# Splitting the weight stream three units ahead, with low parts written over the raw weights

## The chip, the cores and the metric

The kernel runs on one core of a Trainium2 chip. The metric is device time in microseconds (us) of one execution. TensorE (PE) multiplies, PEld is its weight load, VectorE (DVE) and ScalarE (ACT) do elementwise work, GpSimd (POOL) and SyncE (SP) here mostly issue DMA transfers.

## The reference

One token sequence (256 tokens, width 2048) passes through two transformer-like blocks. Nearly all arithmetic is in matrix products with float32 weights:

```python
def first_block(x, ...):
    h = rmsnorm(x, ln1_w)
    z, xbc, dt_raw, q, k, v, f_raw = jnp.split(h @ w_in, split_at, axis=-1)
    x = x + jnp.concatenate([ssd_group(...), fox_group(...)], axis=-1) @ w_out
    x = x + peer(rmsnorm(x, ln2_w), peer_wq, peer_k1, peer_k2, peer_u, peer_v)
    return rmsnorm(x, lnf_w)

def peer(h, wq, k1, k2, u, v):      # 16384 experts, 8 heads, 16 picks each
    s1, s2 = ...                    # scores of h @ wq against two sets of keys
    v1, i1 = lax.top_k(s1, 16); v2, i2 = lax.top_k(s2, 16)
    sc, pos = lax.top_k(all sums v1 + v2, 16)
    act = gelu(u[idx] . h)          # idx: the picked experts
    return sum(softmax(sc) * act * v[idx])

def second_block(x, mem, ...):      # attention + convolution, cross attention, MLP
    h = h + jnp.square(jax.nn.relu(nm @ w1[l])) @ w2[l]
```

The kernel computes the experts' part densely for 208 of the 256 tokens (all 16384 experts, gated by a sparse table) and by gathered rows for the other 48.

## The kernel before, in words

All weight matrices are laid out as one stream of 532 units of 128 x 2048 float32 (1 MB each). A unit gives PE 16 tiles of 128 x 128 to multiply with. To keep float32 accuracy, every unit is split: ACT copies it to a rounded high part (`w_hi`, helper `hi`, line 672; its caller in the units with two matmuls per tile cuts it in 1536 and 512 columns, lines 685 and 691), DVE subtracts to get the low part (`w_lo`, helper `lo`, line 1117), and PE multiplies with both.

Buffers before: `raw` has four slots of 1 MB, `w_hi` and `w_lo` two each. SP loads unit u+4 into the slot of unit u as soon as `split_done` shows unit u split (line 521). ACT and DVE split unit u+2 in the helper `ahead(u)`, which waits for `mm_done` of unit u, since unit u+2 takes the buffers that PE has just finished with. PE waits at the start of each unit for `split_done` and `bank_free`.

Every engine runs its instructions in the order in which the program is written. Stages in the order of the stream, with the stage names of the table `STREAM`: `xbc`, `v1`, `z`, `qk1`, `out1` (first mixing block), `wq` (queries; DVE does the top-k in between), `u0` (first 2048 experts, DVE goes on with the top-k), `u1` (DVE builds the one-hot tiles `pick_a`, `pick_b` for the gate table, PE multiplies them in `gate_group`, ACT evicts them), `e0`, `e1`, then six rounds `u2`, `e2` ... `u7`, `e7`. In those rounds POOL gathers expert rows (1 MB each) for the 48 tokens, two buffers, and DVE handles one gathered block in a `job` at fixed units. `job(0)` stands after unit 3 of `u2` and waits for `set_rows`, two broadcast loads issued at the start of `u2`. In a round's `u` stage ACT copies a bank (L950), applies Gelu (L954) and writes the high part of the gated activation (`cast`, L942), DVE adds (L1601), gates (L1555) and writes the low part (`act_lo`, L1616). In unit 0 of the following `e` stage PE waits tile by tile for them: its tile 15 needs `act_lo` of unit 15 (`gated_tile`). In `e` stages DVE accumulates (L1594, L1595). Then come the stages of the second block, the last eight of which (`up`, `down`) are the MLP.

The order of ACT's work in unit k of a `u` stage is, in full:

```python
ahead_first(u)
eng.wait_ge(mm_done, u + 1)
eng.wait_ge(tmp_split, n - 3)
eng.activation(tmp[:, j, 0:TD], bank[j][:, TD:2 * TD], ACT.Copy).then_inc(pair_copied, 1)
if k < 15:
    ahead_rest(u)
eng.wait_ge(pair_sum, 16 * (r - 2) + k + 1)
eng.activation(tmp[:, j, 0:TD], tmp[:, j, 0:TD], ACT.Gelu).then_inc(tmp_full, 1)
if k >= 1:
    cast(r, k - 1)
if k == 15:
    ahead_rest(u)
    cast(r, 15)
```

Of the kernel before, what the change touches and what calls it, by code (L numbers as in the profile page):

```python
# [21 lines left out]
P = 128  # L22
D = 2048
T = 256
# [5 lines left out]
SPLIT = 2  # L30
# [97 lines left out]
def build(nc, x_in, mem_in, stream, cols_in, consts_in, rows_in, wide_in, wdtf_in, keys_in,  # L128
          rel_in, onehot_in, u_rows, v_rows, out):
    ctx = ExitStack()  # L130
    with ctx:
# [19 lines left out]
        w_hi = [sb(f"w_hi{i}", [P, UNIT], F32R) for i in range(SPLIT)]  # L151
        w_lo = [sb(f"w_lo{i}", [P, UNIT], F32R) for i in range(SPLIT)]
# [131 lines left out]
        mm_part = sem("mm_part")  # L284
# [160 lines left out]
        PART = 3 * UNIT // 4  # L445

# [64 lines left out]
        def _(sp_eng):  # L511
# [154 lines left out]
        def _(act):  # L666
            eng = nc.scalar

            def hi(landed, k):

                eng.wait_ge(raw_full[k % RAW], landed)
                eng.activation(w_hi[k % SPLIT][:, :], raw[:, k % RAW, :], ACT.Copy).then_inc(hi_done, 1)  # L672
# [7 lines left out]
            def ahead_first(u):  # L680

                k = u + 2
                eng.wait_ge(mm_part, u - UNIT0["e0"] + 1)
                eng.wait_ge(raw_full[k % RAW], 16 * (k // RAW + 1))
                eng.activation(w_hi[k % SPLIT][:, 0:PART], raw[:, k % RAW, 0:PART], ACT.Copy)  # L685

            def ahead_rest(u):

                k = u + 2
                eng.wait_ge(mm_done, u + 1)  # L690
                eng.activation(w_hi[k % SPLIT][:, PART:UNIT], raw[:, k % RAW, PART:UNIT], ACT.Copy).then_inc(hi_done, 1)  # L691
# [89 lines left out]
            for j in range(SPLIT):  # L781
                hi(16, j)
# [146 lines left out]
            for name in ("e0", "e1"):  # L929
                for k in range(16):  # L930
                    ahead_first(UNIT0[name] + k)
                    ahead_rest(UNIT0[name] + k)
# [11 lines left out]
            for r in range(2, PEER_ROUNDS):  # L944
                for k in range(16):
                    u, n, j = UNIT0[f"u{r}"] + k, BQ[f"u{r}"] + k, k % 4
                    ahead_first(u)
# [3 lines left out]
                    if k < 15:  # L951
                        ahead_rest(u)
# [4 lines left out]
                    if k == 15:  # L957
                        ahead_rest(u)
# [20 lines left out]
            for j in range(16):  # L979
# [6 lines left out]
                ahead_first(UNIT0["e7"] + j)  # L986
                ahead_rest(UNIT0["e7"] + j)
# [109 lines left out]
            for j in range(14):  # L1097
                ahead(u0 + j)
# [11 lines left out]
        def _(dve):  # L1110
# [135 lines left out]
            for j in range(SPLIT):  # L1246
# [606 lines left out]
            for j in range(16):  # L1853
                if j % 4 == 3:
                    add_chunk((j // 4) * 512, (j // 4) % 2, u0 + j + 1, stat[:, 14:16])
                if j < 14:
# [13 lines left out]
        def _(pe):  # L1870
# [3 lines left out]
            def feature_unit(j, act_t, built=None, between=None, c0=0, c1=T, tile=None, ready=None):  # L1874
                hi, lo = w_hi[j % SPLIT], w_lo[j % SPLIT]
# [16 lines left out]
            def paired_unit(j, both, built=None, between=None, c0=0, c1=T, tile=None, ready=None, part=False):  # L1892

                hi, lo = w_hi[j % SPLIT], w_lo[j % SPLIT]
# [3 lines left out]
                for kt in range(KT):  # L1898
# [8 lines left out]
                    inst = mm(o2, lo[:, ks], pair[:, 0, :], start=False, stop=False, skip_group_check=True)  # L1907
                    if part and (kt + 1) * P == PART:
                        inst.then_inc(mm_part, 1)
# [3 lines left out]

            def part_unit(*args, **kw):
                paired_unit(*args, **kw, part=True)
# [10 lines left out]
            def row_unit(j, banks, act_t, k0, first, end, tile=None, ready=None, between=None):  # L1926
                tile = tile or (lambda half, k: act_t[half][:, k, :])
                hi, lo = w_hi[j % SPLIT], w_lo[j % SPLIT]
# [289 lines left out]
            feature("e0", 16, None, unit=part_unit, tile=e0_pair, c1=TD, ready=lambda kt: eng.wait_ge(a2_ready, Z_TILES + kt + 1))  # L2218
# [322 lines left out]
```

## Time and profile before

| what | value |
|---|---|
| median of 3 runs | 3111.43 us (3110.13 to 3116.72) |
| the profiled execution's own time | 3117.25 us |
| its span, first to last instruction | 3115.5 us |
| PE busy | 3019.5 us (97%) |
| DVE busy | 2258.5 us (72%) |
| ACT busy | 1426.0 us (46%) |
| mean granted TensorE clock | 0.989 of full speed |
| moved by DMA | 705.49 MB, 226 GB/s over the span |

The share of busy time says how full an engine is, not which wait sets the end. Waits are put down to what released them: `PE bank L1906 <- DVE w_lo L1117` is time in which PE stood before a matmul of line 1906 until DVE had written `w_lo`.

### The profile page before, as it was taken

What the parts mean: (1) busy time and instruction counts of PE and PEld (TensorE: products, weight loads), DVE (VectorE), ACT (ScalarE), POOL (GpSimd) and SP (SyncE); (2) the same over time, 40 slices, a digit from 0 to 9 for tenths busy, and PEclk for the clock granted to TensorE, in tenths of its full rate; (3) what the DMA queues carried; (4) which work ended last, traced back from release to release, by engine and by line L of the source; (5) the groups of instructions that cost most, each with busy time, mean ns of one, the idle gap of its engine ahead of it and who ended that gap; (6) DMA issues with size and microseconds to landing.
All of it is one profiled execution on the core that took longest, in us unless ns stands there. A gap on an engine that the chain in (4) does not pass through costs nothing. (4 is left out here: it accounts for less than half of the span.)

```text
span 3115.5 us, 49787 instructions
## 1 busy us (share of the span) xinstructions
PE 3019.5 (97%) x19428; PEld 2808.5 (90%) x19428; DVE 2258.5 (72%) x3201; ACT 1426.0 (46%) x1762; POOL 180.1 (6%) x223
## 2 busy tenths in 40 slices
PE   7999999999997999999999999999999999999998
PEld 7899889999997999999999999999788888888886
DVE  4766559999865889888988877598656646555564
ACT  4465443356443444555454455434444333333333
POOL 1000000020000111111111100000000000000000
PEclk9999999999998999999999999999999999999999
DMA  5443464456768999999999874544444555555553
GB/s 204 175 149 136 150 211 150 166 199 229 255 252 227 339 343 354 342 352 343 356 338 359 315 294 179 182 177 150 162 176 148 185 194 188 189 188 188 188 188 135
DMA packets 101661, 705.49 MB, mean 226 GB/s; under 512 B 13320, under 2 KB 13344, under 8 KB 17728
## 3 DMA queue, kind: packets, MB, share of 16 engines
q1 hardware_dynamic: 77472, 562.07, 50.0%
q0 software_dynamic: 22192, 128.10, 11.9%
q10 hardware_dynamic: 1872, 13.63, 1.1%
q8 instruction: 80, 1.31, 0.2%
q14 instruction: 45, 0.37, 0.0%
HBM read 685.46 MB, written 18.24 MB: 226 GB/s over the span
## 5 line engine op out<-in xcount | busy, mean ns | idle before, releaser
L1117 DVE TENSOR_TENSOR w_lo<-raw,w_hi 128x2048 fp32r<-128x2048 f32 x532 | 1218.5, 2290 | 514.8 <-ACT w_hi L672 489.6
L1906 PE MATMUL bank<-a_both,w_hi 128*128 128x416 f32 (+1 forms) x3840 | 1231.0, 378 | 25.5 <-DVE w_lo L1117 21.8
L1907 PE MATMUL bank<-a_both,w_lo 128*128 128x208 f32 (+1 forms) x4096 | 1042.8, 265 | 0.0
L1906 PEld LDWEIGHTS bank<-a_both,w_hi 128*128 128x128 f32 x3840 | 725.5, 189 | 80.9 <-issue 25.7
L1907 PEld LDWEIGHTS bank<-a_both,w_lo 128*128 128x128 f32 x4096 | 782.6, 191 | 7.2
L672 ACT ACTIVATE w_hi<-raw 128x2048 fp32r<-128x2048 f32 x308 | 588.4, 1911 | 379.8 <-PE bank L1938 361.6
L1884 PE MATMUL bank<-a_both,w_hi 128*128 128x256 f32 (+1 forms) x1984 | 572.9, 289 | 21.0 <-DVE w_lo L1117 13.7
L685 ACT ACTIVATE w_hi<-raw 128x1536 fp32r<-128x1536 f32 x224 | 333.7, 1490 | 523.2 <-PE bank L1907 503.7
L1885 PE MATMUL bank<-a_both,w_hi 128*128 128x256 f32 (+1 forms) x1984 | 560.0, 282 | 0.0
L1886 PE MATMUL bank<-a_both,w_lo 128*128 128x256 f32 (+1 forms) x1984 | 559.9, 282 | 0.0
L1884 PEld LDWEIGHTS bank<-a_both,w_hi 128*128 128x128 f32 x1984 | 383.7, 193 | 28.9 <-issue 11.1
L1885 PEld LDWEIGHTS bank<-a_both,w_hi 128*128 128x128 f32 x1984 | 383.9, 193 | 0.5
L1886 PEld LDWEIGHTS bank<-a_both,w_lo 128*128 128x128 f32 x1984 | 383.5, 193 | 0.0
L1936 PE MATMUL bank<-w_hi,a_both 128*128 128x512 f32 x960 | 377.6, 393 | 2.0 <-DVE a_both L1128 1.5
L1938 PE MATMUL bank<-w_hi,a_both 128*128 128x512 f32 x960 | 373.9, 389 | 0.0
L1937 PE MATMUL bank<-w_lo,a_both 128*128 128x512 f32 x960 | 373.6, 389 | 0.0
L1936 PEld LDWEIGHTS bank<-w_hi,a_both 128*128 128x128 f32 x960 | 180.2, 188 | 40.6 <-DVE a_both L1128 2.2
L1938 PEld LDWEIGHTS bank<-w_hi,a_both 128*128 128x128 f32 x960 | 180.2, 188 | 37.9
L1937 PEld LDWEIGHTS bank<-w_lo,a_both 128*128 128x128 f32 x960 | 180.3, 188 | 36.3
L1906 PE MATMUL bank<-e_both,w_hi 128*128 128x416 f32 x480 | 146.0, 367 | 0.0
L691 ACT ACTIVATE w_hi<-raw 128x512 fp32r<-128x512 f32 x224 | 138.3, 617 | 0.0
L1907 PE MATMUL bank<-e_both,w_lo 128*128 128x208 f32 x512 | 127.1, 258 | 0.0
(327 smaller groups left out, 2529.3 us busy)
## 6 DMA issues: line engine op xcount, KB each, us to landing
raw<-stream_dram SPq DMA_DIRECT2D x532, 1024.0 KB, 4.9
gates_scratch<-stage ACTq DMA_DIRECT2D x13, 1024.0 KB, 4.4
gbuf<-gates_scratch POOLq DMA_DIRECT2D x30, 416.0 KB, 7.3
x<-x_dram SPq DMA_DIRECT2D x2, 1024.0 KB, 6.5
x_scratch<-x POOLq DMA_DIRECT2D x1, 2048.0 KB, 11.0
set_rows<-xw_scratch POOLq DMA_DIRECT2D x2, 1024.0 KB, 22.9
mem<-mem_dram POOLq DMA_DIRECT2D x1, 2048.0 KB, 9.7
xm<-x_scratch POOLq DMA_DIRECT2D x1, 2048.0 KB, 12.5
```

Of the source, the lines that this page charges most:

```text
L672: eng.activation(w_hi[k % SPLIT][:, :], raw[:, k % RAW, :], ACT.Copy).then_inc(hi_done, 1)
L685: eng.activation(w_hi[k % SPLIT][:, 0:PART], raw[:, k % RAW, 0:PART], ACT.Copy)
L691: eng.activation(w_hi[k % SPLIT][:, PART:UNIT], raw[:, k % RAW, PART:UNIT], ACT.Copy).then_inc(hi_done, 1)
L1117: eng.tensor_tensor(w_lo[k % SPLIT][:, :], raw[:, k % RAW, :], w_hi[k % SPLIT][:, :].bitcast(F32), ALU.subtract).then_inc(split_done, 1)
L1884: mm(o, hi[:, ks], tile(0, kt), start=kt == 0, stop=False)
L1885: mm(o, hi[:, ks], tile(1, kt), start=False, stop=False)
L1886: last = mm(o, lo[:, ks], tile(0, kt), start=False, stop=kt == KT - 1)
L1906: mm(o, hi[:, ks], pair, start=kt == 0, stop=False)
L1907: inst = mm(o2, lo[:, ks], pair[:, 0, :], start=False, stop=False, skip_group_check=True)
L1936: mm(o, tile(0, k0 + k)[:, ts], hi[:, ns], start=first and k == 0, stop=False)
L1937: mm(o, tile(0, k0 + k)[:, ts], lo[:, ns], start=False, stop=False)
L1938: last = mm(o, tile(1, k0 + k)[:, ts], hi[:, ns], start=False, stop=end and k == 3)
```

## The change

The two low buffers are gone: DVE writes the low part into the slot of `raw` that it reads. The room goes to two more high buffers, so that there are four slots of raw/low and four of high. `ahead(u)` now splits unit u+3 and no longer waits for `mm_done`; ACT waits only for the unit's data. SP's refill of a slot waits for `mm_done` of the unit in it, since PE reads the low part there. The cut of the high copy in two (`ahead_first`, `ahead_rest`, semaphore `mm_part`) is gone.

```diff
 RAW = 4
-SPLIT = 2
+AHEAD = 3
@@
-        w_hi = [sb(f"w_hi{i}", [P, UNIT], F32R) for i in range(SPLIT)]
-        w_lo = [sb(f"w_lo{i}", [P, UNIT], F32R) for i in range(SPLIT)]
+        raw_at = base[0] - RAW * UNIT * 4
+        w_hi = [sb(f"w_hi{i}", [P, UNIT], F32R) for i in range(RAW)]
+        raw_lo = at("raw_lo", [P, RAW, UNIT], F32R, raw_at)
+        w_lo = [raw_lo[:, i, :] for i in range(RAW)]
@@ SP
-                    eng.wait_ge(split_done, g * RAW + (j - RAW + 1))
+                    eng.wait_ge(mm_done, g * RAW + (j - RAW + 1))
@@ ACT
             def ahead(u, *loops):
-                k = u + 2
-                eng.wait_ge(mm_done, lin(u + 1, *loops))
+                k = u + AHEAD
                 hi(lin(16 * (k // RAW + 1), *((v, n * 16 // RAW) for v, n in loops)), k)
@@ ACT, rounds
-                    ahead_first(u)
                     eng.wait_ge(mm_done, u + 1)
                     eng.wait_ge(tmp_split, n - 3)
                     eng.activation(tmp[:, j, 0:TD], bank[j][:, TD:2 * TD], ACT.Copy).then_inc(pair_copied, 1)
                     if k < 15:
-                        ahead_rest(u)
+                        ahead(u)
@@
                     if k == 15:
-                        ahead_rest(u)
+                        ahead(u)
                         cast(r, 15)
@@
                 for k in range(16):
-                    ahead_first(UNIT0[f"e{r}"] + k)
-                    ahead_rest(UNIT0[f"e{r}"] + k)
+                    ahead(UNIT0[f"e{r}"] + k)
@@ DVE
-                eng.tensor_tensor(w_lo[k % SPLIT][:, :], raw[:, k % RAW, :], w_hi[k % SPLIT][:, :].bitcast(F32),
+                eng.tensor_tensor(w_lo[k % RAW], raw[:, k % RAW, :], w_hi[k % RAW][:, :].bitcast(F32),
                                   ALU.subtract).then_inc(split_done, 1)
             def ahead(u, *loops):
-                lo(lin(u + 3, *loops), u + 2)
+                lo(lin(u + AHEAD + 1, *loops), u + AHEAD)
```

What stands on ACT at the end of a `u` stage of the rounds (units 14 and 15 of `u2`, then the first units of `e2`), before:

```order
L950 ACTIVATE tmp_61<-bank2 128x208 [waits tmp_split,mm_done]
L691 ACTIVATE w_hi0_50<-raw_49 128x512 [waits mm_done]
L954 ACTIVATE tmp_61<-tmp_61 128x208 [waits pair_sum]
L942 ACTIVATE a2_both_55<-tmp_61 128x208 [waits g_used]
L685 ACTIVATE w_hi1_51<-raw_49 128x1536 [waits raw_full1,mm_part]
L950 ACTIVATE tmp_61<-bank3 128x208 [waits tmp_split,mm_done]
L954 ACTIVATE tmp_61<-tmp_61 128x208 [waits pair_sum]
L942 ACTIVATE a2_both_55<-tmp_61 128x208 [waits g_used]
L691 ACTIVATE w_hi1_51<-raw_49 128x512 [waits mm_done]
L942 ACTIVATE a2_both_55<-tmp_61 128x208 [waits g_used]
```

and of the change, at the same place:

```order
L933 ACTIVATE tmp_62<-bank2 128x208 [waits tmp_split,mm_done]
L671 ACTIVATE w_hi1_51<-raw_49 128x2048 [waits raw_full1]
L937 ACTIVATE tmp_62<-tmp_62 128x208 [waits pair_sum]
L926 ACTIVATE a2_both_56<-tmp_62 128x208 [waits g_used]
L933 ACTIVATE tmp_62<-bank3 128x208 [waits tmp_split,mm_done]
L937 ACTIVATE tmp_62<-tmp_62 128x208 [waits pair_sum]
L926 ACTIVATE a2_both_56<-tmp_62 128x208 [waits g_used]
L671 ACTIVATE w_hi2_52<-raw_49 128x2048 [waits raw_full2]
L926 ACTIVATE a2_both_56<-tmp_62 128x208 [waits g_used]
```

The last gated high part (`a2_both`, the last row) stood behind a quarter of a high copy whose data was there; it now stands behind a whole copy that waits for its load.

What stands on DVE around `job(0)` (the `got_137` row, here an ISA instruction), before:

```order
L1601 TENSOR_TENSOR tmp_61<-tmp_61,bank3 128x208 [waits pair_copied]
L1117 TENSOR_TENSOR w_lo1_53<-raw_49,w_hi1_51 128x2048 [waits pair_sum,hi_done]
L1555 TENSOR_TENSOR tmp_61<-tmp_61,gbuf_102 128x208 [waits tmp_full]
L1616 TENSOR_TENSOR a2_both_55<-tmp_61,a2_both_55 128x208 [waits act_hi]
L1631 ISA got_137,row_dot_69<-got_137,set_rows0_140 128x2048 [waits s_got0,s_rows]
```

and of the change:

```order
L1583 TENSOR_TENSOR tmp_62<-tmp_62,bank3 128x208 [waits pair_copied]
L1099 TENSOR_TENSOR raw_lo_54<-raw_49,w_hi2_52 128x2048 [waits pair_sum,hi_done]
L1537 TENSOR_TENSOR tmp_62<-tmp_62,gbuf_103 128x208 [waits tmp_full]
L1598 TENSOR_TENSOR a2_both_56<-tmp_62,a2_both_56 128x208 [waits act_hi]
L1613 ISA got_138,row_dot_70<-got_138,set_rows0_141 128x2048 [waits s_got0,s_rows]
```

The places are the same; the split ahead of the job is that of unit 5 of `u2` before (`w_hi1`) and of unit 6 now (`w_hi2`).

## Rows read from the trace of the kernel before

**Rows 1.** The page: busy time by engine, costliest groups (busy, mean ns | idle).

```profile
span 3115.5 us, 49787 instructions
PE 3019.5 (97%) x19428; PEld 2808.5 (90%) x19428; DVE 2258.5 (72%) x3201; ACT 1426.0 (46%) x1762; POOL 180.1 (6%) x223
...
L1117 DVE TENSOR_TENSOR w_lo<-raw,w_hi 128x2048 fp32r<-128x2048 f32 x532 | 1218.5, 2290 | 514.8 <-ACT w_hi L672 489.6
...
L672 ACT ACTIVATE w_hi<-raw 128x2048 fp32r<-128x2048 f32 x308 | 588.4, 1911 | 379.8 <-PE bank L1938 361.6
L685 ACT ACTIVATE w_hi<-raw 128x1536 fp32r<-128x1536 f32 x224 | 333.7, 1490 | 523.2 <-PE bank L1907 503.7
```

**Rows 2.** PE's waits over the whole span (total us, times, longest).

```profile
PE bank L1906 <- DVE w_lo L1117: 21.8, 8, 11.2
...
PE bank L1884 <- DVE w_lo L1117: 13.7, 10, 2.9
PE bank L2203 <- DVE pick_a L1537: 4.9, 5, 1.7
```

**Rows 3.** Busy time by stretch: wq/u0, start of u2, u3.

```profile
546.00:624.00 78.00, 73.12 (x612) 71.62 (x611) 73.95 (x169) 28.81 (x28) 0.00 (x0) 0.96 0.48 171
...
936.00:1014.00 78.00, 61.26 (x375) 59.81 (x375) 43.77 (x49) 30.91 (x51) 6.67 (x7) 0.87 0.84 226
...
1170.00:1248.00 78.00, 77.66 (x514) 76.47 (x513) 69.56 (x77) 38.97 (x57) 11.71 (x12) 1.00 0.95 355
```

**Rows 4.** DVE's timeline in u0: low parts that it waited for.

```profile
588.59 2.29 DVE L1117 TENSOR_TENSOR w_lo<-raw,w_hi 128x2048 fp32r<-128x2048 f32 x1 [0.81 <-ACT w_hi L672]
594.21 2.29 DVE L1117 TENSOR_TENSOR w_lo<-raw,w_hi 128x2048 fp32r<-128x2048 f32 x1 [2.25 <-ACT w_hi L672]
...
646.66 2.29 DVE L1117 TENSOR_TENSOR w_lo<-raw,w_hi 128x2048 fp32r<-128x2048 f32 x1 [3.43 <-ACT w_hi L672]
```

**Rows 5.** Timeline of POOL and ACT at the start of u2.

```profile
943.63 1.40 POOL L626 DMA_DIRECT2D set_rows<-xw_scratch  x2 [68.61 <-PE bank L1912]
...
968.42 1.48 ACT L685 ACTIVATE w_hi<-raw 128x1536 fp32r<-128x1536 f32 x1 [8.95 <-DMA raw<-stream_dram]
...
978.08 1.49 ACT L685 ACTIVATE w_hi<-raw 128x1536 fp32r<-128x1536 f32 x1 [6.87 <-DMA raw<-stream_dram]
```

**Rows 6.** Tile set_rows, 940 to 1000; tile raw, 956 to 958: issue and landing.

```profile
DMA to landing us min/median/max: 4.4/22.9/41.4
...
L521 SPq DMA_DIRECT2D raw<-stream_dram x1: 333/333/333, 956.6 to 956.6; - x1
...
DMA to landing us min/median/max: 26.1/26.1/26.1
```

**Rows 7.** DVE's timeline in u2: the first job and the split behind it.

```profile
985.79 2.29 DVE L1631 CUSTOM_DVE_ANT_0 got<-got,set_rows 128x2048 f32<-128x2048 f32 x1 [12.24 <-DMA set_rows<-xw_scratch]
...
988.52 2.29 DVE L1117 TENSOR_TENSOR w_lo<-raw,w_hi 128x2048 fp32r<-128x2048 f32 x1
```

**Rows 8.** PE's waits, 1040 to 1100 and 1794 to 1980.

```profile
PE bank L1906 <- DVE w_lo L1117: 3.3, 1, 3.3
...
PE bank L1884 <- DVE w_lo L1117: 2.0, 1, 2.0
```

**Rows 9.** Tile raw, 1092 to 1716: time from issue to landing, 128 loads.

```profile
L521 SPq DMA_DIRECT2D raw<-stream_dram x128: 332/333/333, 1095.3 to 1713.2; - x128
...
DMA to landing us min/median/max: 4.7/7.1/10.2
```

**Rows 10.** Timelines at the end of u4: PE's last matmuls of units; ACT; DVE.

```profile
1358.61 0.36 PE L1912 MATMUL bank<-a_both,w_hi 128*128 128x416 f32 x1
1363.41 0.37 PE L1912 MATMUL bank<-a_both,w_hi 128*128 128x416 f32 x1
...
1361.01 0.36 ACT L942 ACTIVATE a_both<-tmp 128x208 fp32r<-128x208 f32 x1
...
1361.40 0.37 DVE L1616 TENSOR_TENSOR a_both<-tmp,a_both 128x208 fp32r<-128x208 f32 x1 [0.40 <-ACT a_both L942]
```

More of the change, by code:

```diff
@@ L671, in hi @@
                 eng.wait_ge(raw_full[k % RAW], landed)
-                eng.activation(w_hi[k % SPLIT][:, :], raw[:, k % RAW, :], ACT.Copy).then_inc(hi_done, 1)
+                eng.activation(w_hi[k % RAW][:, :], raw[:, k % RAW, :], ACT.Copy).then_inc(hi_done, 1)
             def ahead(u, *loops):
-                k = u + 2
-                eng.wait_ge(mm_done, lin(u + 1, *loops))
+                k = u + AHEAD
                 hi(lin(16 * (k // RAW + 1), *((v, n * 16 // RAW) for v, n in loops)), k)
[L680 to L691, printed above, removed]
             def feature(name, n, first, evict, r=None, unroll=False):
@@ L780, in _ @@
                 scaled_tile("ln1", kt)
-            for j in range(SPLIT):
+            for j in range(AHEAD):
                 hi(16, j)
@@ L930, in _ @@
                 for k in range(16):
-                    ahead_first(UNIT0[name] + k)
-                    ahead_rest(UNIT0[name] + k)
+                    ahead(UNIT0[name] + k)
             def row_gelu():
@@ L985, in _ @@
                     part_square(1, xm, (j - 8) // 4)
-                ahead_first(UNIT0["e7"] + j)
-                ahead_rest(UNIT0["e7"] + j)
+                ahead(UNIT0["e7"] + j)
                 if j < TT:
@@ L1096, in _ @@
             u0 = UNIT0[f"down{FF_ROUNDS - 1}"]
-            for j in range(14):
-                ahead(u0 + j)
+            for j in range(16):
+                if j + AHEAD < 16:
+                    ahead(u0 + j)
                 if j in (8, 9, 12):
@@ L1245, in _ @@
             eng.tensor_tensor(wd[1][:, :, :], wdtf[:, :, :], wd[0][:, :, :].bitcast(F32), ALU.subtract).then_inc(wd_done, 1)
-            for j in range(SPLIT):
+            for j in range(AHEAD):
                 lo(j + 1, j)
@@ L1855, in _ @@
                     add_chunk((j // 4) * 512, (j // 4) % 2, u0 + j + 1, stat[:, 14:16])
-                if j < 14:
+                if j + AHEAD < 16:
                     ahead(u0 + j)
@@ L1874, in feature_unit @@
             def feature_unit(j, act_t, built=None, between=None, c0=0, c1=T, tile=None, ready=None):
-                hi, lo = w_hi[j % SPLIT], w_lo[j % SPLIT]
+                hi, lo = w_hi[j % RAW], w_lo[j % RAW]
                 tile = tile or (lambda half, k: act_t[half][:, k, c0:c1])
@@ L1890, in feature_unit, with paired_unit @@
                         between(kt)
-            def paired_unit(j, both, built=None, between=None, c0=0, c1=T, tile=None, ready=None, part=False):
-                hi, lo = w_hi[j % SPLIT], w_lo[j % SPLIT]
+            def paired_unit(j, both, built=None, between=None, c0=0, c1=T, tile=None, ready=None):
+                hi, lo = w_hi[j % RAW], w_lo[j % RAW]
                 tile = tile or (lambda k: both[:, k, :, c0:c1])
@@ L1906, in paired_unit @@
                         mm(o, hi[:, ks], pair, start=kt == 0, stop=False)
-                    inst = mm(o2, lo[:, ks], pair[:, 0, :], start=False, stop=False, skip_group_check=True)
-                    if part and (kt + 1) * P == PART:
-                        inst.then_inc(mm_part, 1)
+                    mm(o2, lo[:, ks], pair[:, 0, :], start=False, stop=False, skip_group_check=True)
                     if between:
@@ L1927, in row_unit @@
                 tile = tile or (lambda half, k: act_t[half][:, k, :])
-                hi, lo = w_hi[j % SPLIT], w_lo[j % SPLIT]
+                hi, lo = w_hi[j % RAW], w_lo[j % RAW]
                 for k in range(4):
@@ L2217, in _ @@
                 feature_unit(k, a1, between=between, c0=G)
-            feature("e0", 16, None, unit=part_unit, tile=e0_pair, c1=TD, ready=lambda kt: eng.wait_ge(a2_ready, Z_TILES + kt + 1))
-            feature("e1", 16, None, unit=part_unit, tile=e1_pair, c1=TD, ready=lambda kt: eng.wait_ge(e1_ready, kt + 1))
+            feature("e0", 16, None, unit=paired_unit, tile=e0_pair, c1=TD, ready=lambda kt: eng.wait_ge(a2_ready, Z_TILES + kt + 1))
+            feature("e1", 16, None, unit=paired_unit, tile=e1_pair, c1=TD, ready=lambda kt: eng.wait_ge(e1_ready, kt + 1))
             def gated_tile(name, r):
@@ L2268, in _ @@
                 eng.wait_ge(bank_free, 4 * ROUND0["e7"] + j + 1)
-                part_unit(j, a2_both, c1=TD, ready=gated_tile("u7", None) if j == 0 else None)
+                paired_unit(j, a2_both, c1=TD, ready=gated_tile("u7", None) if j == 0 else None)
             def last_acc(kt):
```

10 lines of the change are left out of this document (3 added, 7 removed).

## The prediction

> **What bounds the kernel now.** I read the page first: of a span of 3115.5 us PE is busy for 3019.5 [rows 1], so all of PE's idle time is 3115.5 - 3019.5 = 96 us, and no better feed of weights can give more. PE's waits say which part of it is a late split: 21.8 us in eight waits in the units with two matmuls per tile, one of them 11.2 us long, and 13.7 us in ten waits in those with three [rows 2], 35.5 us together. The rest waits for norms, activations and gate tiles, which the change doesn't make.
>
> Then the windows, to see where these waits lie and what else is full there [rows 3]. From 546 to 624 us DVE is busy for 73.95 of 78 us (top-k) and PE for 73.12: DVE is the pace-maker. From 936 to 1014 us PE is idle for 78 - 61.26 = 16.7 us at a granted clock of 0.87; the DMA engines are busy for 0.84 but move only 226 GB/s. From 1170 to 1248 us, one slice of the long rounds (u2 to e7, 192 units), PE is busy for 77.66 of 78, DVE for 69.56, and the DMA engines for 0.95 at 355 GB/s. There is nothing to win there and something to lose.
>
> The landing times of the weight loads complete the picture: in the rounds 4.7 us at least, 7.1 in the median, 10.2 at most [rows 9]. A unit takes 1363.41 - 1358.61 = 4.80 us there [rows 10], the rounds some 922 us.
>
> **What the change does to the two slacks.** Work out the loop for one slot in the rounds. Before, the split of unit u+2 begins when PE ends unit u and must be done one unit later: slack is 4.8 us for the rest of the high copy, 2.3 us of low part [rows 1] and whatever DVE is busy with. The load, though, is issued right after the unit four earlier is split, nearly five units before PE needs it. After, the load of unit u+4 is issued at PE's end of unit u; landing, 1.9 us of high copy and 2.3 us of low part [rows 1] must fit in three units, 14.4 us. With the median landing: 0.1 + 7.1 + 1.9 + 2.3 = 11.4, leaving 3.0 us for DVE's other work, more than the 4.8 - 3.5 = 1.3 us that it has now (the last quarter of the copy, by 1911 less 1490 ns [rows 1] some 0.5, handing over, 2.3). With the worst landing: 0.1 + 10.2 + 1.9 + 2.3 = 14.5, which is 0.1 over. So slack against a busy DVE grows where loads land fast, and slack against slow loads shrinks: six different units are held in the buffers before, four after.
>
> **Part by part.**
>
> (a) *Top-k stages, 468 to 765 us.* DVE works back to back here, so a deeper lead makes no time as such; what counts is time in which DVE itself stood. It stood for 0.81, 2.25 and 3.43 us, each time for ACT's high copy, which waited for PE's end of the unit [rows 4]. Now PE may be one unit further on before it needs a given split, its evictions and the high copies behind them come earlier, and DVE, being late, finds its copy done. The sum is 6.5 us. PE's own waits for w_lo there end, but it then stands before the picks and gate tiles (L2203 waits already now, 4.9 us [rows 2]), which DVE hands out 6.5 us earlier and no more. I take -6.5; bounds 0 (the waits come back at another place of DVE's order) and -11 (most of the 13.7 us [rows 2]).
>
> (b) *Start of u2.* set_rows is issued at 943.63 [rows 5] and its slower half takes 41.4 us [rows 6], to about 985. Loads of weights crawl beside it: the data of unit 5 of u2 comes at 968.4, of unit 6 at 978.1 [rows 5], of unit 7 at 956.6 + 26.1 = 982.7 [rows 6]. Then job(0) holds DVE until 985.79 and the split of unit 6 follows at 988.52 [rows 7], so that PE takes up unit 6 at 990.8. After the change refills are asked for later, by more than a unit; at the time when set_rows begins the load in flight is that of unit 3, not 4. I take the crawling queue's deliveries as they are and shift them by one: unit 4 at 968.4, 5 at 978.1, 6 at 982.7. With 4.2 us of split, PE starts unit 5 at 982.3 and unit 6 at 987.1, which now stands ahead of the job on DVE. Unit 7's split is behind the job: 987 (low part of 6), 0.7 for two short ones, 2.4 for the job, 0.5, 2.3, is 992.9, against 990.8 + 4.8 = 995.6 at the earliest before. That is 3 us, and with the lowered clock of 0.87 in this stretch [rows 3] lifting a little I take -4. Bounds: -10 if the clock stays up and loads come a bit earlier; +10 if the whole loss of two units of store (2 x 4.8 = 9.6) comes out as a stall.
>
> The share that the weight queue gets beside set_rows is what the shift rests on: unit 7's load takes 26.1 us against a least 4.7 in the rounds [rows 6, 9]. The Trainium skill (DMA: Bandwidth & Descriptors, Queues, rings and completion order) says that each DMA engine takes turns between its queues, a packet at a time; by that the share doesn't depend on how many loads SP has outstanding, and the shift by one holds; the rows agree so far as a slow queue delivers one unit after the other.
>
> (c) *Other late splits.* 21.8 - 16.7 = 5.1 us of the first kind lie outside that window [rows 2, 3], 3.3 of them in one wait after the three jobs in a row at the end of u2, and another 2.0 us of the second kind come at 1794 to 1980 [rows 8]. A lead of one more unit covers each: -7.1. Bounds -8.5 and -3.
>
> (d) *Turns from u to e.* A new wait. The last gated high part stands on ACT behind the high copy for unit u+3. Before, it began at 1361.01 and DVE's low part at 1361.40, done at 1361.8, 2.8 us after PE's end of the unit, 1358.97 [rows 10]; PE needs it 15/16 of a unit in, at +4.5. After: the load is issued at -4.7, lands at +2.4, copy to +4.3, cast 0.36 to +4.7, DVE with handing over to +5.2: PE stands for 0.7 us. There are six such turns, and e0 to e1 has the same shape (its last tile is behind DVE's split): 7 x 0.7 = +4.9. Bounds: 0 with landings below 6.4, and 7 x (10.2 - 7.1 + 0.7) = +27 with the slowest landing of [rows 9] at each.
>
> (e) *Slow landings elsewhere in the rounds.* At 10.2 us the loop is 0.1 over, and DVE's jobs (2.3 us) can lie before the split. I charge one such meeting in each of six rounds at 0.3: +2. Bounds 0 and +10.
>
> *At nothing:* two instructions of high copy become one (1490 ns and the quarter, now 1911 [rows 1]); ACT has room, 38.97 of 78 us busy in the fullest slice [rows 3]. The low part written in place reads and writes as much as before. The third split ahead of the first stage hides under the wait for the first products; uncovered it would cost 1.9 + 2.3 = 4 us once. In the MLP stages PE has no wait that a split ends.
>
> Sum: -6.5 - 4 - 7.1 + 4.9 + 2 = -10.7. The profiled execution took 3117.25 us, which is 5.8 above the median of the runs, 3111.43; from the median the forecast is 3100.7, say **3101 us**.
>
> **Rivals.** *The loads become the bound (slower).* In the rounds DMA is at 0.95 [rows 3]. If refills that start at PE's end collide with the gathers so that landings pass 14.4 - 0.1 - 4.2 = 10.1 us, each unit is longer by a third of the excess: with 11.0 us in 100 of the 192 units it is 100 x 0.9 / 3 = +30, with the turns at 11.0 another 7 x 4.6 = 32 less what stalls give back. A milder form, landings of 10.2 at all turns and at the slow places, gives 27 + 10 - 17.6 = +19: 3131. Against it: the queue has the same bytes to carry, asked for at an even beat, and 7.1 leaves 3.0 us. It decides from a median of about 9 us. I give the mild form as the time of this rival, 3125 to 3135, chance 0.17. The Trainium skill (DMA: Bandwidth & Descriptors, Rules for kernel authors) says to issue a DMA early and wait for it late; the change does the opposite by up to two units, and by this rule alone it would be slower; the time is the one just worked out from rows.
>
> *The lead is worth little (no change).* DVE still waits in the top-k stages at other places, (a) is 0, and the start of u2 costs as much as it gives: 0 + 0 - 7.1 + 4.9 + 2 = 0: 3111. For it: PE is 97% busy, and the chain in the top-k stages is DVE's. Chance 0.20.
>
> *More is won (faster still).* No landing is slow at the turns, (d) and (e) are 0, (b) is -10: -6.5 - 10 - 7.1 = -24: 3088. Chance 0.13.
>
> **How the numbers follow.** The forecast has 0.50, with a range of its own of 3094 to 3108. About 0.2%, 6.2 us, is what can be told from no change: from 3105.2 to 3117.6. Of the forecast 0.42 lies below, 0.08 within; of the second rival 0.03 below, 0.14 within, 0.03 above; the third lies below with 0.13; of the first 0.15 above, 0.02 within. Faster 0.58, same 0.24, slower 0.18. The range leaves out some 0.08 at the bottom and 0.12 at the top: 3088 to 3122.
>
> **What would show it.** PE's waits for w_lo fall from 35.5 to below 12 us. DVE's waits for w_hi between 580 and 650 us are gone and the first gate group starts 6 us earlier. In u2 DVE's low part ahead of job(0) is that of unit 6, and PE's idle time from 936 to 1014 falls from 16.7 to about 13, in more and shorter pieces. New waits of PE for a_both (L1616) at six turns, 0.7 each. ACT waits for raw in every unit of the rounds, about 2 us. Landings stay near 7.1; if they are at 9 or above, the first rival is right and the forecast wrong. It would also be wrong if job(0)'s hole grows, that is if the loads beside set_rows are later by more than one place.

## The result, and the profile after

The changed kernel takes 3133.48 us (median of 5 runs, 3128.86 to 3139.61), the kernel before, run beside it, 3111.43. The ratio is 1.007, with a 95% interval of 1.0059 to 1.0081: slower by 22 us, where the forecast was 10 us faster, 3101 us, with 3122 as the upper end of its range. The two profiled executions stand 16.2 us apart (3133.48 against 3117.25), and what is split into stages below adds up to 16.1 of those. One execution of an experiment's kernel (the lead of two) took 9314 us at a mean granted clock of 0.351; it is left out of the numbers below, and its trace is not read.

Page of the changed kernel: span, busy time and the two split groups (out<-in, shapes, count | busy us, mean ns | idle before, releaser).

```profile
span 3131.7 us, 49084 instructions
...
PE 3028.5 (97%) x19428; PEld 2814.5 (90%) x19428; DVE 2247.8 (72%) x3201; ACT 1404.4 (45%) x1538; POOL 179.6 (6%) x223
...
L1099 DVE TENSOR_TENSOR raw_lo<-raw,w_hi 128x2048 fp32r<-128x2048 f32 x532 | 1218.0, 2290 | 656.5 <-ACT w_hi L671 645.5
L671 ACT ACTIVATE w_hi<-raw 128x2048 fp32r<-128x2048 f32 x532 | 1017.4, 1913 | 858.1 <-DMA raw<-stream_dram 760.5
```

The low part takes 2290 ns over the raw weights as it did beside them [rows 1]. DVE stands 156 us longer for high copies (645.5 against 489.6), and ScalarE no longer stands for PE but for the load. PE is itself busy 9.0 us longer for the same 19428 matmuls: part of them ran slower.

PE's waits of the changed kernel, whole span (us, times, longest).

```profile
PE bank L1888 <- DVE raw_lo L1099: 18.0, 13, 11.9
...
PE bank L1888 <- DVE a_both L1598: 8.6, 10, 3.4
PE bank L1889 <- DVE a_both L1598: 8.5, 6, 1.5
PE bank L1866 <- DVE raw_lo L1099: 5.5, 3, 2.9
...
PE bank L1944 <- DVE a_both L1116: 4.1, 4, 2.9
...
PE bank L2169 <- DVE picked L1495: 2.7, 1, 2.7
```

Waits for low parts of weights fell from 35.5 us [rows 2] to 23.5. The waits for low parts of the activations (L1598), are 17.1; the kernel before has none for the same tiles (its L1616).

Windows of the changed kernel, the same three as in [rows 3], in the same columns.

```profile
546.00:624.00 78.00, 72.52 (x613) 72.01 (x614) 76.90 (x170) 29.25 (x27) 0.00 (x0) 0.96 0.48 174
936.00:1014.00 78.00, 63.51 (x396) 61.80 (x395) 43.33 (x51) 30.18 (x39) 6.70 (x8) 0.91 0.83 238
1170.00:1248.00 78.00, 74.75 (x481) 72.74 (x480) 66.86 (x74) 36.18 (x40) 11.16 (x11) 0.98 0.90 329
```

In the top-k stages DVE is now full (76.90 of 78); at the start of u2 PE's idle time falls from 16.7 to 14.5 us; in a slice of the rounds PE is idle for 3.25 us where it was for 0.34. The DMA engines do less there, not more.

PE's event at the end of each unit gives the stages' lengths. The table is worked out from these events of two executions each: us that a group of stages takes more than in the kernel before. Executions of one kernel differ among themselves (3107.97 to 3116.72 before, 3128.86 to 3139.61 changed), so an entry of 1 or 2 us says little. The last two columns are experiments, told below.

```
stages             changed   lead of two (again)   mixed lead
ahead of wq          +0.3         -1.4                +0.1
wq, u0               -8.7         +1.0                -9.0
u1                   +2.9         +0.4                +1.9
e0, e1               +3.3         +0.9                +0.8
u2                   -3.4         -2.6                -2.8
e2                   +1.8         -4.0                -4.5
u3 to u6             +3.3        +12.1                +2.0
e3 to e6            +15.8         +4.6                +1.3
u7                   -0.8         +0.6                -0.8
e7                   +7.6         -0.3                -0.5
ck to the end        -6.1         -1.4                -3.1
sum                 +16.1         +9.8               -14.7
```

So the loss is in the e stages, most of it in their first units. Timeline of the changed kernel at the end of u5 (start, us, engine, operation [idle before, releaser]); PE ends unit 14 at 1516.0 and unit 15 at 1521.0. DVE first:

```profile
1521.81 0.36 DVE L1583 TENSOR_TENSOR tmp<-tmp,bank 128x208 f32<-128x208 f32 x1
1522.32 2.29 DVE L1099 TENSOR_TENSOR raw_lo<-raw,w_hi 128x2048 fp32r<-128x2048 f32 x1
...
1524.81 0.37 DVE L1598 TENSOR_TENSOR a_both<-tmp,a_both 128x208 fp32r<-128x208 f32 x1
...
1526.20 0.37 DVE L1598 TENSOR_TENSOR a_both<-tmp,a_both 128x208 fp32r<-128x208 f32 x1
1528.23 0.38 DVE L1598 TENSOR_TENSOR a_both<-tmp,a_both 128x208 fp32r<-128x208 f32 x1 [1.67 <-ACT a_both L926]
```

ScalarE:

```profile
1519.18 1.92 ACT L671 ACTIVATE w_hi<-raw 128x2048 fp32r<-128x2048 f32 x1 [1.65 <-DMA raw<-stream_dram]
...
1526.04 1.90 ACT L671 ACTIVATE w_hi<-raw 128x2048 fp32r<-128x2048 f32 x1
1527.84 0.36 ACT L926 ACTIVATE a_both<-tmp 128x208 fp32r<-128x208 f32 x1
```

PE:

```profile
1525.23 0.46 PE L1888 MATMUL bank<-a_both,w_hi 128*128 128x416 f32 x1 [0.34 <-DVE a_both L1598]
...
1526.62 0.46 PE L1888 MATMUL bank<-a_both,w_hi 128*128 128x416 f32 x1 [0.83 <-DVE a_both L1598]
...
1528.67 0.43 PE L1889 MATMUL bank<-a_both,raw_lo 128*128 128x208 f32 x1 [1.49 <-DVE a_both L1598]
1528.89 0.59 PE L1892 MATMUL bank<-a_both,w_hi 128*128 128x416 f32 x1
```

DVE's addition for unit 14 (L1583) comes at 1521.81, 5.8 us behind PE's end of that unit, so the low tiles 13, 14 and 15 all come late, and the last one stands for a high copy of 1.90 us besides. In the kernel before, the last tile began at +2.4 us after PE's end of the unit [rows 10]; here it begins at +7.2. PE then also slows down:

```profile
1527.00:1530.00 3.00, 1.51 (x7) 1.30 (x6) 1.76 (x2) 3.00 (x3) 0.76 (x1) 0.80 0.87 290
1530.00:1533.00 3.00, 3.00 (x15) 2.93 (x14) 2.97 (x4) 0.01 (x1) 0.00 (x0) 0.63 0.91 281
1533.00:1536.00 3.00, 3.00 (x22) 2.98 (x21) 3.00 (x3) 0.48 (x1) 0.00 (x0) 1.00 0.30 120
```

In these windows of the changed kernel the granted clock is 0.80 and then 0.63, that is partly at the lower of its two levels (1.2 GHz), behind 2.7 us of standing in three pieces. The first unit of e5 takes 8.47 us (before 4.80), the second 6.13 (before 5.40). At the turn to e4 the first unit takes 8.17 us and the second only 4.80; there the clock did not fall.

The 7.6 us of e7 lie at two places. Its first two units take 8.19 and 9.78 us (before 6.58 each), 4.8 us in all. The seventh takes 8.56 us (before 5.25): PE stands 2.9 us there for a scaled tile of the memory's norm (L1116), whose high part ScalarE (L722) makes behind two high copies that wait for their loads:

```profile
1877.34 1.92 ACT L671 ACTIVATE w_hi<-raw 128x2048 fp32r<-128x2048 f32 x1 [8.39 <-DMA raw<-stream_dram]
1880.74 1.92 ACT L671 ACTIVATE w_hi<-raw 128x2048 fp32r<-128x2048 f32 x1 [1.48 <-DMA raw<-stream_dram]
1882.57 0.81 ACT L722 ACTIVATE a_both<-bank,cols 128x256 fp32r<-128x256 f32 x2
```

### The profile page after: what moved, and what is told of

Its sections match the earlier page's. It is cut to its first block, busy times and chain, and to the rows that moved or that the text cites. A ratio compares the mean times of both kernels' runs of the same rounds, so it can differ in the third digit from the quotient of the medians.

```text
span 3131.7 us, 49084 instructions
## 1 busy us (share of the span) xinstructions
PE 3028.5 (97%) x19428; PEld 2814.5 (90%) x19428; DVE 2247.8 (72%) x3201; ACT 1404.4 (45%) x1538; POOL 179.6 (6%) x223
## 4 chain that ended last, share of the span: by engine, by line
PE 73%; DVE 16%; DMA 5%; ACT 3%; issue 2%; POOL 0%; SPq 0%; ACTq 0%; DVEq 0%
PE bank L1888 23%; PE bank L1889 12%; PE bank L1913 6%; PE bank L1915 6%; PE bank L1914 6%; DVE raw_lo L1099 6%; PE bank L1866 5%; PE bank L1868 5%; PE bank L1867 5%; DMA raw<-stream_dram 5%; ACT w_hi L671 2%; PE bank L1892 2%; DVE pick_a L1519 2%; DVE pick_b L1514 1%; DVE got L1613 1%
## 5 line engine op out<-in xcount | busy, mean ns | idle before, releaser
L1099 DVE TENSOR_TENSOR raw_lo<-raw,w_hi 128x2048 fp32r<-128x2048 f32 x532 | 1218.0, 2290 | 656.5 <-ACT w_hi L671 645.5
L671 ACT ACTIVATE w_hi<-raw 128x2048 fp32r<-128x2048 f32 x532 | 1017.4, 1913 | 858.1 <-DMA raw<-stream_dram 760.5
L1889 PE MATMUL bank<-a_both,raw_lo 128*128 128x208 f32 (+1 forms) x4096 | 1046.1, 265 | 8.5 <-DVE a_both L1598 8.5
L1889 PEld LDWEIGHTS bank<-a_both,raw_lo 128*128 128x128 f32 x4096 | 784.5, 192 | 17.3 <-DVE a_both L1598 10.1
L1868 PE MATMUL bank<-a_both,raw_lo 128*128 128x256 f32 (+1 forms) x1984 | 560.8, 283 | 0.0
L1868 PEld LDWEIGHTS bank<-a_both,raw_lo 128*128 128x128 f32 x1984 | 384.5, 194 | 0.0
L1914 PE MATMUL bank<-raw_lo,a_both 128*128 128x512 f32 x960 | 373.6, 389 | 0.0
L1914 PEld LDWEIGHTS bank<-raw_lo,a_both 128*128 128x128 f32 x960 | 180.3, 188 | 36.7
L1889 PE MATMUL bank<-e_both,raw_lo 128*128 128x208 f32 x512 | 127.4, 259 | 1.3 <-DVE e_both L1564 1.3
L1071 ACT ACTIVATE tmp<-bank 128x256 f32<-128x256 f32 x64 | 24.7, 386 | 219.2 <-PE bank L1892 218.7
L1613 DVE CUSTOM_DVE_ANT_0 got<-got,set_rows 128x2048 f32<-128x2048 f32 x48 | 109.7, 2285 | 2.0 <-DMA got<-u_rows_dram,row_idx 2.0
## 6 DMA issues: line engine op xcount, KB each, us to landing
mem<-mem_dram POOLq DMA_DIRECT2D x1, 2048.0 KB, 10.1
```

Source lines behind the costliest of these rows:

```text
L671: eng.activation(w_hi[k % RAW][:, :], raw[:, k % RAW, :], ACT.Copy).then_inc(hi_done, 1)
L1099: eng.tensor_tensor(w_lo[k % RAW], raw[:, k % RAW, :], w_hi[k % RAW][:, :].bitcast(F32), ALU.subtract).then_inc(split_done, 1)
L1613: inst = eng.tensor_tensor_reduce(rows_got, rows_got, rows_set[:, :], 1.0, 0.0, ALU.mult, ALU.add, row_dot[:, n:n + 1])
L1868: last = mm(o, lo[:, ks], tile(0, kt), start=False, stop=kt == KT - 1)
L1914: mm(o, tile(0, k0 + k)[:, ts], lo[:, ns], start=False, stop=False)
```

## The experiments

Each kernel ran beside the kernel before (medians of 3112.1 to 3114.3 in the four groups). Theory T blames the turns, theory R the late loads; both stand in full in the expectations. The first four:

**The cast ahead of the copy.**

```diff
                     if k == 15:
-                        ahead(u)
                         cast(r, 15)
+                        ahead(u)
```

> Theory T (the loss is at the turns from u to e: with a lead of three units DVE reaches the last units of a u stage some 5 us behind PE, and ScalarE's whole high copy of 1.8 us, which waits for its own load, stands ahead of the last cast): with the cast of tile 15 put ahead of that copy the last cast comes about 1.7 us sooner at each of six turns, so some 8 to 10 us less than the changed kernel, 3124; the first unit of e3 to e6 ends 1 to 1.7 us sooner each. Rival R (the loss comes from the later refill: loads issued when PE ends a unit land late): nothing moves, 3133. Rival D (DVE's backlog alone sets the last tiles, the copy on ScalarE is beside it): under 3 us, 3131.

Measured: 3123.0 us, ratio 1.0033 (1.0020 to 1.0046), some 10 us less than the changed kernel, as T said. The waits of its PE from 1126 to 1830 us (u3 to u7, without u7's last units):

```profile
PE bank L1888 <- DVE a_both L1598: 4.7, 8, 0.8
PE bank L1888 <- DVE raw_lo L1099: 2.7, 6, 0.7
```

The same stretch of the changed kernel has 10.6 us of waits for L1598. The first two units of e5 take 6.71 and 4.80 us, and the clock stays at 1.00 from 1521 to 1536 us. What is left of the turn is DVE's delay. In e7 the first two units take 6.58 us each, as in the kernel before, but the seventh takes 11.95 us, with a wait of 4.5 us for its tile (L1116) and a clock of 0.50: that loss did not go with the cast, it grew.

**Jobs early.**

```diff
-        JOBS = {"u": (1, 3, 5, 6, 8, 10, 11, 13), "e": (0, 2, 3, 5, 6, 8, 10, 11, 13, 14)}
+        JOBS = {"u": (0, 1, 3, 4, 6, 7, 9, 10), "e": (0, 2, 3, 5, 6, 8, 10, 11, 13, 14)}
```

> The eight gather jobs of DVE in u3 to u6 stand at units 0, 1, 3, 4, 6, 7, 9, 10 and no longer at 1, 3, 5, 6, 8, 10, 11, 13, so that DVE has five units without one ahead of the turn; u2 and the turn to e2 are as before, a control. T: DVE's additions of u3 to u6 are within 2 us of PE's ends again at unit 14, the first two units of e3 to e6 lose 2 to 3.5 us less each, and the kernel takes 8 to 14 us less than the changed kernel, about 3122; e2's first unit doesn't move. Rival R (late loads): 3133. Rival O (it is ScalarE's order and not DVE's backlog that sets the turn): under 3 us less, 3131.

Measured: 3135.63 us, ratio 1.0084 (1.0066 to 1.0102): nothing gained, against T. The trace says why. DVE at the end of u5 in this kernel (PE ends unit 14 at 1509.7, unit 15 at 1514.5):

```profile
1512.32 0.36 DVE L1583 TENSOR_TENSOR tmp<-tmp,bank 128x208 f32<-128x208 f32 x1
1515.70 2.29 DVE L1099 TENSOR_TENSOR raw_lo<-raw,w_hi 128x2048 fp32r<-128x2048 f32 x1 [3.02 <-ACT w_hi L671]
```

and ScalarE:

```profile
1513.75 1.92 ACT L671 ACTIVATE w_hi<-raw 128x2048 fp32r<-128x2048 f32 x1 [3.49 <-DMA raw<-stream_dram]
1515.57 0.36 ACT L937 ACTIVATE tmp<-tmp 128x208 f32<-128x208 f32 x1
```

Free of jobs, DVE had come up to 2.6 us behind PE at unit 14. Then it stood for 3.02 us, for a copy that had stood for its load; the GELU of unit 14 stood behind that copy too. The last low tile of the activations began 7.1 us behind PE's end of unit 15, where it was 7.2. At this turn it is the load that holds both engines back, not the jobs.

**A lead of two.**

```diff
-AHEAD = 3
+AHEAD = 2
```

> The changed kernel with a lead of two units; four high buffers, low parts in place and the refill at PE's end stay. T: PE's short waits for low parts come back (some 30 us over the kernel), and they keep DVE in step with PE, so the turns cost what they cost in the kernel before: 3113 to 3120, with the first unit of e3 to e6 at 4.8 to 6 us again. Rival R (the refill at PE's end is what costs): 3130 or more, since loads have one unit less ahead of a split that still comes early. Rival I (writing in place slows the subtraction or something beside it): 3130, with no stage better than in the changed kernel.

Measured: 3132.54 us, ratio 1.0071 (1.0057 to 1.0084), where T had 3113 to 3120: the lead alone is not the loss. The trace of this kernel comes from its second run, below.

**Late refill alone**, in the kernel before.

```diff
-                    eng.wait_ge(split_done, g * RAW + (j - RAW + 1))
+                    eng.wait_ge(mm_done, g * RAW + (j - RAW + 1))
```

> The kernel before with one edit: SyncE's refill of a raw buffer waits for PE's end of the unit and not for the split. It prices the later refill alone. T: loads land 4 to 5 us later but still ahead of most splits; 2 to 6 us more than the kernel before, 3113 to 3117, spread over the places where a landing takes over 9 us. Rival R: 15 us or more, 3127 or above, as in the changed kernel.

Measured: 3119.43 us, ratio 1.0018 (1.0009 to 1.0027). The later refill costs some 6 us, a little above the 3117 that T allowed, and not R's 15.

**The activations' chain ahead of the split** at units 13 to 15, on both engines, under theory T2. The diff shows ScalarE's side; the last cast also goes ahead of the copy, and DVE's order changes in the same way.

```diff
-                    if k < 15:
+                    if k < 13:
                         ahead(u)
...
+                    if k >= 13:
+                        ahead(u)
```

> The changed kernel with, at units 13, 14 and 15 of u2 to u7, GELU and cast ahead of the high copy on ScalarE, and gating and low part of the activations ahead of the weights' subtraction on DVE. Theory T2, formed after the first four runs (moving jobs away did nothing, and in both traces DVE's addition for unit 14 runs over 5 us behind PE's end of it): DVE and ScalarE are held behind PE by the loads themselves, since the split of unit u+3 stands right behind the addition of unit u, and its load was issued only at PE's end of unit u-1, 4.8 us earlier, and lands after 7. Then this order frees the last three tiles from that wait: the first two units of e3 to e6 take 10 to 11 us together and not 14 to 14.6, last low tiles within 3.5 us of PE's end, and the kernel takes 3114 to 3119. Rival B (DVE is simply full, 4.6 of 4.8 us a unit, and late whatever the order): gains as with the cast alone, 3123. Rival R: 3133.

Measured: 3143.18 us, ratio 1.0103 (1.0088 to 1.0118): 10 us worse than the changed kernel, where 3114 to 3119 was expected. PE waits 20.5 us for the last activations (L1599 here) instead of 17.1. DVE of this kernel at the end of u4 (PE ends unit 14 at 1360.1, unit 15 at 1365.3):

```profile
1363.41 2.29 DVE L1100 TENSOR_TENSOR raw_lo<-raw,w_hi 128x2048 fp32r<-128x2048 f32 x1 [1.41 <-ACT w_hi L671]
...
1367.83 0.37 DVE L1584 TENSOR_TENSOR tmp<-tmp,bank 128x208 f32<-128x208 f32 x1
...
1370.71 2.29 DVE L1100 TENSOR_TENSOR raw_lo<-raw,w_hi 128x2048 fp32r<-128x2048 f32 x1 [1.41 <-ACT w_hi L671]
```

The split of one unit had only changed places with the chain of its own unit; it still stands ahead of the next unit's addition (which comes 7.8 us behind PE's end of unit 14), with a wait of 1.41 us of its own that the chain had covered. My edit tested the order badly: it did not take the last tiles out from behind the loads.

**A lead of two, cast first.** `AHEAD = 2` and the edit of the first experiment together.

> The changed kernel with a lead of two units and the last cast ahead of the copy. With a lead of two a load is issued 9.6 us ahead of its place on DVE, so T2 has DVE in step here, and what the version with a lead of two lost at the turns can only be the whole copy of 1.9 us ahead of the last cast (before it was a last quarter of 0.6): the first two units of e3 to e6 take under 11 us together, and the time falls from 3134 to 3120 to 3124. Rival I (the low parts written in place, or a whole copy with the loads so late, cost all over the e stages): 3130 or more, with waits for low parts of 25 us or over.

Measured: 3131.84 us, ratio 1.0064 (1.0050 to 1.0078). The edit that gave 10 us at a lead of three gives nothing here; the expectation failed. Waits of PE from 1126 to 1830 us:

```profile
PE bank L1888 <- DVE raw_lo L1099: 14.6, 26, 1.3
```

There is no wait for activations left, so DVE is in step at the turns, as T2 has it. What remains in this stretch are 26 short waits for low parts of weights.

**Low parts in place**, in the kernel before, with the late refill. The diff shows the new buffers; the room of the old `w_lo` stays empty, and every use of `w_lo` takes the slot of `raw`.

```diff
+        raw_lo = at("raw_lo", [P, RAW, UNIT], F32R, raw_at)
+        w_lo = [raw_lo[:, i, :] for i in range(RAW)]
```

> The kernel before with the low parts written over the raw weights and the refill at PE's end; two high buffers and the copy in two parts stay. Against the run with the late refill alone (3119.4) it prices writing in place. T2: nothing, 3118 to 3121, with DVE's subtraction at 2.29 us as before. Rival I: 3127 or more, by a longer subtraction or by slower matrix products beside it.

Measured: 3116.47 us, ratio 1.0010 (1.0001 to 1.0019), its interval overlapping that of the late refill alone (1.0009 to 1.0027). Writing in place costs nothing that can be told.

**The lead of two once more, and with the copy first.** The first is `AHEAD = 2` alone. The second, against the changed kernel:

```diff
-AHEAD = 3
+AHEAD = 2
...
+                    ahead(u)
                     eng.wait_ge(mm_done, u + 1)
                     eng.wait_ge(tmp_split, n - 3)
                     eng.activation(tmp[:, j, 0:TD], bank[j][:, TD:2 * TD], ACT.Copy).then_inc(pair_copied, 1)
-                    if k < 15:
-                        ahead(u)
...
                     if k == 15:
-                        ahead(u)
                         cast(r, 15)
```

> The changed kernel with a lead of two and nothing else, once more, for its profile. T3: time as before, 3131 to 3137; the first two units of e3 to e6 take 11 to 13 us together, PE waits for the last low activations at the turns under 8 us in all (17.1 in the changed kernel), and the u stages take 3 us more each than in the kernel before. If the waits at the turns are as in the changed kernel (15 us or more), the copy ahead of the cast makes them by itself and the lead has no part in them.

> The changed kernel with a lead of two units and the whole high copy of unit u+2 at the head of ScalarE's work for unit u in u2 to u7, ahead of the wait for PE's end of u. Four high buffers allow it. Theory T3, formed after the run with a lead of two and the last cast first (no wait for activations left at the turns, but 3 us more in every u stage and 37 waits for low parts instead of 13): with a lead of two the loss is the copy's place, 1.9 us in one piece behind PE's end, where the kernel before had 0.6 of it; DVE then waits 1.2 us more in every unit of a stage in which it works 4.6 of 4.8 us. So here the u stages give back their 3 us, the waits for low parts are 25 to 30 us again, and the time is that of the run with low parts in place, 3113 to 3119. Rival R2 (a lead of two needs the old refill whatever ScalarE does): 3127 or more.

Measured: 3131.17 us, ratio 1.0059 (1.0044 to 1.0073), for the first, and 3113.61, ratio 1.0005 (0.9996 to 1.0013), for the second. Both times came out as expected: where the one copy stands is worth 18 us. PE's waits for low parts in the version with the copy first are 36.9 us over the span (before 35.5), more than the 25 to 30 expected, but 2.6 of them from 1126 to 1830 us. DVE's subtractions from 1126 to 1830 us, with its idle time ahead of them, in the lead of two:

```profile
L1099 DVE TENSOR_TENSOR raw_lo<-raw,w_hi 128x2048 fp32r<-128x2048 f32 x141 | 322.5, 2287 | 51.4 <-ACT w_hi L671 46.7
```

with the copy first:

```profile
L1097 DVE TENSOR_TENSOR raw_lo<-raw,w_hi 128x2048 fp32r<-128x2048 f32 x144 | 329.4, 2288 | 12.6 <-ACT w_hi L671 1.1 <-DVE tmp L1581 0.5
```

and in the changed kernel:

```profile
L1099 DVE TENSOR_TENSOR raw_lo<-raw,w_hi 128x2048 fp32r<-128x2048 f32 x141 | 322.9, 2290 | 92.6 <-ACT w_hi L671 85.0
```

**A mixed lead.** With the copy first as in the last edit, a lead of three up to u1 and of two from e0 on:

```diff
+                if u == SHORTER:
+                    return
-                k = u + AHEAD
+                k = u + (3 if u < SHORTER else 2)
```

> The changed kernel with a lead of three up to u1, one split left out at u1's last unit, a lead of two from e0 on, and the copy at the head of ScalarE's work in u2 to u7. T3: the 5.5 us that the lead of three has won by the end of u1 stay, and the rounds cost what they cost in the run before this one: some 5 us under it, 3108 to 3113, no slower than the kernel before. If the gain of the top-k stages is given back at e0 or u2 (a wait for something that is late by itself), it is the same as the run with a lead of two all through, 3113 to 3119.

Measured: 3107.4 us, ratio 0.9977 (0.9968 to 0.9987): faster than the kernel before by 7 us and than the changed kernel by 26. The gain of the top-k stages stays (last column of the table).

**Fewer transfers**, in the changed kernel and in the kernel before. The gathers after the first two are left out, and with them the experts' part of the 48 tokens; DVE's jobs stay and run on the rows of the first two. The diff shows the gather alone.

```diff
                             eng.wait_ge(got_used, n + 1)
-                            gather(n + 2)
```

> The changed kernel without the 94 gathers of rows after the first two (1 MB each); DVE's jobs stay at their places and take as long, on rows that stand there already and with a factor of zero, so the PEER part of 48 tokens is left out. Theory T2 (with a lead of three DVE and ScalarE are late at the turns because the load of unit u+3 is issued only 4.8 us before its split stands next on DVE): weights land in the rounds after 5 to 6 us and not 7, DVE's addition for unit 14 comes 2 us nearer to PE's end, PE's waits for the last low activations fall from 17.1 to 8 us or less, and the distance to the same edit of the kernel before falls from 20 us to 10 or less. Rival B (DVE is full by its own work, whatever the loads do): waits of 14 us or more, distance of 17 us or more.

> The kernel before with the same edit, the other end of that distance; it leaves out the same part of the computation. T2 and B alike: its splits are seldom late in the rounds, so it gains little, 3100 to 3110.

Measured: 3114.5 us, ratio 1.0007 (0.9998 to 1.0016), and 3109.67, ratio 0.9991 (0.9982 to 1.0000). The distance between the two kernels is 4.8 us where it was 22. In the changed kernel without gathers the weights land thus (tile raw, 1108 to 1732 us; 4.6/6.9/10.1 with them):

```profile
DMA to landing us min/median/max: 4.6/4.8/7.4
```

and PE's waits from 1126 to 1830 us are

```profile
PE bank L1888 <- DVE a_both L1597: 6.0, 4, 1.5
```

against 10.6 with the gathers (8.7 over the span, a little above the 8 expected). The distance is what is left after the gains of the other stages: by single executions e3 to e6 still take 8.7 us more than in the kernel before (15.8 with the gathers), and e7 7.5 more (7.6). So faster landings take away nearly half of the loss in e3 to e6 and none of that in e7; ScalarE's whole copy still stands ahead of the last cast.

## Why the prediction was wrong

**What held.**

- *Part (a)*, top-k stages: wq and u0 are 8.7 us shorter (forecast 6.5), DVE's three waits for high copies between 580 and 650 us [rows 4] are gone, and its first group of gate tiles starts at 646.72 instead of 652.55. But u1 gives 2.9 back: PE now stands 2.7 us for the picks (L2169; 0.8 before). DVE hands them out 6.2 us earlier, as the forecast said, and PE is there 8.7 us earlier. Net -5.8.
- *Part (b)*, start of u2: -3.4 against -4, in the way that was forecast: the low part of unit 6 is done at 984.9 us, ahead of `job(0)`, where it began at 988.52 before [rows 7], and PE takes up unit 7 at 993.0 (forecast 992.9).
- *Part (c)*, other late splits, -7.1, held in part: ck is 3.6 us shorter, where 2.0 us of late splits had been seen; of the 3.3 us in e2 nothing is seen, since that turn got its own wait (up to 3.4 us for L1598). The other gain from ck on, 2.6 us in `up0`, is no late split: the profiled execution of the kernel before ran at a clock of 0.51 from 2393 to 2400 us, the changed one at 1.00 from 2392 to 2400. That the sum of these stages comes near the forecast is luck.
- *At nothing*, in place: right, by the run of it alone.
- *Part (e)*: u3 to u6 are 3.3 us longer against 2.
- *The first rival* (the loads grow slower) did not happen: landings are 4.6/6.9/10.1 us, before 4.7/7.1/10.2 [rows 9]. Its time, 3125 to 3135, is the one that was measured, but what it named as the sign, landings of about 9 us, is absent; the time came about in another way.

**The step that failed is part (d), the turns from u to e, at +4.9.** Its mechanism was half right (a high copy that waits for its load stands ahead of the last cast) and its size was wrong: e2 to e6 cost 17.6 us and e7 7.6; only the turn from e0 to e1, 1.5 us in e1's first unit, is near its 0.7. The step counts only ScalarE's delay at the one last tile, with DVE in step with PE. That came from the slack: "leaving 3.0 us for DVE's other work". The 3.0 us are slack for PE, which takes up the split three units later; they say nothing of what stands behind the split in DVE's order. There it is the gating and low part of the same unit's activations and the addition of the next. The split of unit u+3 stands on DVE at unit u, but its load is issued only at PE's end of unit u-1. With the median landing, 0.1 + 6.9 + 1.9 us until the copy is done, DVE cannot begin it before 8.9 - 4.8 = 4.1 us after PE's end of unit u, and with the slowest landing 7.3. DVE, whose own work in u stages is by estimate from these rows 16 x 3.4 + 8 x 2.3 = 73 of 77 us, cannot make that up. In the middle of a stage nobody minds, since PE needs no activation of that stage; at the turn it needs all sixteen tiles. The prediction saw ScalarE's wait ("about 2 us in every unit") and did not follow it to what was queued behind it on either engine.

The runs show the links of this chain. Jobs moved away from the turn: DVE runs into the load and stands 3.02 us. The copy put behind the cast: -10 us. A lead of two, with loads 9.6 us ahead of their place on DVE: no wait for activations at the turns at all. Faster landings: the distance shrinks from 22 to 4.8 us. In e7 the first two units' 4.8 us went with the cast's place. The seventh unit's 3.3 us did not, nor with faster landings (8.56 us again); with a lead of two it takes 5.48. That it is the high copy waiting for its load ahead of the scaled tile is read from the trace above and was not tried by itself.

The Trainium skill (DMA: Bandwidth & Descriptors, Rules for kernel authors) has the rule to issue early and wait late. The prediction weighed it and took its price from landings alone. The traces agree with the rule, but at another place: the wait that comes too early is that of ScalarE and DVE for the split, whose turn on DVE comes 4.8 us behind the issue of its load.

**A second step failed unseen: "two instructions of high copy become one", at nothing because "ACT has room".** ScalarE has room, but the kernel before did three quarters of the copy ahead of PE's end of the unit, so that from 1126 to 1830 us DVE stood for only 1.4 us for its copies. In one piece behind PE's end it stands for 46.7 us with a lead of two, and PE waits 26 times. With that lead this costs 18 us over the kernel. In the changed kernel the two causes overlap: 10 us of it went with the cast's place, and how the rest divides wasn't tried. Four high buffers allow the copy to be done before PE's end; the changed kernel does not use that, and with a lead of three could hardly, since half of the loads land 2.1 us or more behind PE's end (6.9 - 4.8).

The later refill, added to the kernel before, cost some 6 us alone and 3 to 4 with the low parts in place; the forecast had 2 for it in part (e). It is not a price that must be paid: the lead of two with the copy first refills as late and can't be told from the kernel before (1.0005).

## What to carry to other kernels

A deeper lead moves an instruction earlier in every queue that it stands in, while the buffers decide how early its data can be there; compare the issue of the load with the instruction's turn on its engine, not with the time at which the result is needed, and ask what is queued behind it. A delay that nobody waits for inside a stage is paid at the stage's end, where the next one needs the last result first. And a lead need not be one number: three units where the splitting engine sets the pace, two where the transfers do, with the copy ahead of PE's end, took 0.23% less than the kernel before. Two throughout with the same copy was level with it, and three throughout, as the change has it, took 0.7% more.

## What the chip showed unasked

An fp32r result written over its own f32 operand costs DVE nothing (2290 ns both ways). Short stands in a row were enough to bring TensorE to its lower level for a while: 0.34, 0.83 and 1.49 us, with one or two matmuls between them, and then matmuls of 0.59 us instead of 0.36 and a granted clock of 0.63 in the next 3 us; with stands of at most 0.8 us (cast first) it stayed at 1.00 there. At the turn to e7 a single stand of 1.35 us was followed by a clock of 0.51 and 0.50 in the 6 us from 1853, and the second unit took 9.78 us instead of 6.58.
